# Stick-breaking keys on both partition halves: two score products of a unit in different rows of the array

## The chip, the cores and the metric

The kernel runs on one core of one Trainium2 chip. The time is device microseconds from the start to the end of one execution. Before the change three runs took 1735.06, 1747.95 and 1748.23 us, median 1747.95. The profiled execution took 1738.63 us, its span from the first to the last instruction 1736.7 us. Engines are called by their short names: PE is TensorE (matrix products and transposes), ACT is ScalarE, DVE is VectorE, POOL is GpSimd, SP issues DMAs.

## The reference

One layer of a hybrid encoder for 1,024 prompt rows and 64 sample rows. The rows are normed and projected to 2,464 columns. Three groups of heads read those columns; their outputs are joined, projected, added to the input, and followed by a gated MLP. The change lies in the third group, four heads of stick-breaking attention with 64 columns each:

```
zz = einsum("bqhd,bkhd->bhqk", q, k) * 64 ** -0.5
mask = k_pos < q_pos
log_beta = log_sigmoid(zz)
log_1mb = where(mask, log_beta - zz, 0)
after = cumsum(log_1mb, reverse=True) - log_1mb
w = where(mask, exp(log_beta + after), 0)
out = einsum("bhqk,bkhd->bqhd", w, v)
```

The prompt attends to itself. The sample's 64 rows attend to 512 cached keys and to their own 64. The sum over d, the inner dimension of the first product, has 64 terms: on PE this product uses 64 of the 128 rows of the array. All of it is fp32.

## The kernel before, in words

The program has three stages: norm and input projection (to 328 us), attention (328 to 800 us), output projection and MLP (the rest). Only the attention stage changes. Its order is written out by hand. There are nine turns: turn 0 is the sample, turns 1 to 8 are the prompt blocks of 128 queries. In turn n the prompt block looks at n x 128 keys, so turns 5 to 8 have more than 512 keys; they are called wide here. Each turn has twelve units, one per head: eight of the softmax group (M) and four stick-breaking (S), in the order S M M S M M S M M S M M.

Each unit passes through steps on all engines. In a step PE makes the scores of one unit (`scores`, lines 2001 to 2027), weighs the values of an earlier one (`weigh`, line 2071), transposes the weights of one between them (`transposes`, line 2051), and does one of twelve front pieces of the next turn (`front`). A front piece turns projected columns of the next block into the layouts that its units need. Piece 0 of each front transposes stick-breaking queries and keys into one PSUM bank; ACT copies the queries to `sqT` (line 1083), and DVE, after ACT, copies the keys to `skT` (line 1516). PE's next front pieces wait until both have read the bank where they share it. On ACT the copies of a front piece stand at the end of a step, ahead of the next step's exponentials and logarithms (lines 1135 to 1143) and of the copies of transposed weights (line 1163) that `weigh` on PE waits for. Before the first turn DVE copies the cached keys to `skT` (line 1481).

`sqT` and `skT` keep two heads on partitions 0 to 63 and two on partitions 64 to 127 (head h on half h % 2, at index h // 2). A score product reads keys and queries of one half. Since a product has at most 512 columns, a unit with more keys has two, into neighbouring PSUM banks, both from the half of its head. Turn 0 has two as well, 512 and 64 keys. A fp32 product leaves two weight-load records and two product records in the trace.

Before each front ACT squares and sums two column ranges of the next block into the two parts of a scratch tile `junk` (lines 1058 and 1060), and then makes their inverse roots.

Of the kernel before, what the change touches and what calls it, by code (L numbers as in the profile page):

```python
# [20 lines left out]
P = 128  # L21
# [154 lines left out]
def key_col(n):  # L176

    return P * SEQ[n]


# [94 lines left out]
def build(nc, I, O, stop_after=None):  # L275
# [4 lines left out]
    with ctx:  # L280
# [85 lines left out]
        qnT = s3("qnT", [3, P])  # L366
        junk = s3("junk", [QR + KVR])
        sums = s3("sums", [2])
# [12 lines left out]
        v_mla = s3("v_mla", [NTILE, 512])  # L381
        skT = s3("skT", [2, T])
        sv = s3("sv", [NTILE, 256])
        qT = s3("qT", [2, H_MLA, P])
        sqT = s3("sqT", [2, 2, P])
        prob = s3("prob", [3, 1024])
# [513 lines left out]
        def _(act):  # L900
# [150 lines left out]
            def prepare(m):  # L1051
# [4 lines left out]
                if m:  # L1056
                    act.wait_ge(s_lat, m)
                act.activation(junk[:r, :QR], x[:, O_ZQ:O_ZQ + QR], ACT.Square, scale=QR ** -0.5,
                               accum_out=sums[:r, 0:1])
                ch.link(act.activation(junk[:r, QR:], x[:, O_KV:O_KV + KVR], ACT.Square, scale=KVR ** -0.5,  # L1060
                                       accum_out=sums[:r, 1:2]))
# [3 lines left out]
            def front(m, p):  # L1065
# [16 lines left out]
                if s == 0:  # L1082
                    last = act.activation(sqT[:, slot, :, :r], v4[:, 0:2, :r], ACT.Copy, scale=SB_SCALE)
                elif s == 1:
# [217 lines left out]
        def _(dve):  # L1302
# [177 lines left out]
            dve.wait_ge(s_cT, 2)  # L1480
            dve.tensor_copy(skT[:, :, 512:1024], psum[:, 2:4, :]).then_inc(s_cD, 1)

# [21 lines left out]
            def front(m, p):  # L1504
# [10 lines left out]
                if s == 0:  # L1515
                    last = dve.tensor_copy(skT[:, :, col:col + r], v4[:, 2:4, :r])
                elif s in (2, 3):
# [256 lines left out]
        def _(pe):  # L1774
# [225 lines left out]
            def scores(i):  # L2000
# [17 lines left out]
                for a in range(0, w, 512):  # L2018
                    b = min(w, a + 512)
                    out = score_bank(i, w)[:r, a:b]  # L2020
                    if kind == "M":
                        last = pe.matmul(out, qT[:QD, slot, h, :r], kT[:QD, h, first + a:first + b],  # L2022
                                         start=True, stop=True)
                    else:
                        lo = 64 * (h % 2)
                        last = pe.matmul(out, sqT[lo:lo + 64, slot, h // 2, :r],  # L2026
                                         skT[lo:lo + 64, h // 2, first + a:first + b], start=True, stop=True)
                last.then_inc(s_sc, 1)
# [191 lines left out]
```

## Time and profile before

| what | value |
|---|---|
| runs | 1735.06, 1747.95, 1748.23 us |
| profiled execution | 1738.63 us, span 1736.7 us |
| mean granted clock of PE | 0.970 |
| busy PE / DVE / ACT / POOL | 1661.3 / 1063.3 / 609.0 / 169.8 us |
| stick-breaking score products (line 2026) | 112 records, 372.6 to 785.0 us |
| query copies `sqT` / key copies `skT` | 9 / 9, and 1 of the cached keys |

Busy time is the time in which an engine executed. A granted clock of 1.00 is PE's 2.4 GHz, 0.50 is 1.2 GHz. The chain of waits is followed back from the last instruction: at each step to what released it, or to the instruction ahead of it on its engine. An instruction with "idle before" had its engine waiting that long for the named releaser.

### The profile page before, as it was taken

The page shows a single profiled execution, that of the slowest core. Times are in us where ns is not written, and L with a number is a line of the kernel's source. Part 1 is how long each engine was busy: PE and PEld are TensorE (multiplying, and loading weights), DVE is VectorE, ACT ScalarE, POOL GpSimd, SP SyncE. Part 2 cuts the span into 40 slices and gives each one's busy share as a digit, 9 for nine tenths or more (in the row PEclk, how much of TensorE's full clock was granted, in tenths as well). Part 3 has the DMA queues.
Part 4 walks back from the last instruction along what each step waited for, and adds up shares of the span by engine and source line. Part 5 has one row for each costly group of instructions (what it writes and reads, how often), then busy time and mean ns, then how long its engine had stood idle before and what let it go on. Part 6 is the DMA issues. An engine that isn't in the chain of part 4 may idle for free.

```text
span 1736.7 us, 27549 instructions
## 1 busy us (share of the span) xinstructions
PE 1661.3 (96%) x10050; PEld 1497.0 (86%) x10050; DVE 1063.3 (61%) x2316; ACT 609.0 (35%) x1199; POOL 169.8 (10%) x226
## 2 busy tenths in 40 slices
PE   6899999899899999999998999999999999999996
PEld 3599999646676777777997999999999999999996
DVE  3766555346776676666327666665666666566657
ACT  4621000235666666666225222121212222121213
POOL 0011111212322212111210000000000000000000
PEclk8999999879988999999999999999999999999999
DMA  9545555511211110016210211111111211111003
GB/s 329 192 157 154 170 157 160 183 39 36 66 48 48 48 36 17 13 49 219 86 37 16 70 37 49 37 43 53 36 48 36 60 36 48 36 36 60 12 1 116
DMA packets 114221, 133.61 MB, mean 77 GB/s; under 512 B 14954, under 2 KB 91545, under 8 KB 112793
## 3 DMA queue, kind: packets, MB, share of 16 engines
q1 hardware_dynamic: 110809, 121.76, 22.0%
q0 software_dynamic: 3328, 10.73, 1.7%
q8 instruction: 53, 0.87, 0.2%
q14 instruction: 31, 0.25, 0.0%
HBM read 107.47 MB, written 27.23 MB: 78 GB/s over the span
## 4 chain that ended last, share of the span: by engine, by line
PE 86%; DVE 5%; ACT 5%; issue 3%; DMA 1%; SPq 0%; ACTq 0%; DVEq 0%; POOLq 0%
PE psum L2102 34%; PE psum L2166 15%; PE psum L1868 13%; PE psum L2071 6%; PE psum L2022 3%; PE psum L2051 3%; PE psum L2026 2%; PE psum L1954 2%; PE psum L1896 1%; PE psum L1901 1%; PE psum L1934 1%; PE psum L1782 1%; DVE h_lo L1422 1%; ACT pT L1163 1%; PE psum L1804 1%
## 5 line engine op out<-in xcount | busy, mean ns | idle before, releaser
L2102 PE MATMUL psum<-act_hi,wt_parts 128*128 128x362 f32 (+1 forms) x2496 | 614.4, 328 | 9.4 <-DVE act_lo L1422 5.2
L1718 DVE SCALAR_TENSOR_TENSOR residual<-psum,mod,residual 128x364 f32<-128x364 f32 (+2 forms) x704 | 299.7, 494 | 257.7 <-PE psum L2166 257.6
L2102 PEld LDWEIGHTS psum<-act_hi,wt_parts 128*128 128x128 f32 x2496 | 441.4, 189 | 12.1 <-issue 6.8
L2102 PE MATMUL psum<-act_lo,wt_parts 128*128 128x362 f32 (+1 forms) x1248 | 408.3, 327 | 0.0
L2166 PE MATMUL psum<-u_hi,wt_parts 128*128 128x362 f32 (+1 forms) x1056 | 263.3, 330 | 3.0 <-issue 3.0
L2102 PEld LDWEIGHTS psum<-act_lo,wt_parts 128*128 128x128 f32 x1248 | 235.0, 188 | 0.0
L2166 PEld LDWEIGHTS psum<-u_hi,wt_parts 128*128 128x128 f32 x1056 | 188.1, 189 | 3.3 <-issue 3.3
L1868 PE MATMUL psum<-w_hi,h_hi 128*128 128x308 f32 (+1 forms) x576 | 177.3, 308 | 3.9 <-DVE h_lo L1422 2.1
L1868 PE MATMUL psum<-w_lo,h_hi 128*128 128x308 f32 (+1 forms) x576 | 175.9, 305 | 0.0
L1868 PE MATMUL psum<-w_hi,h_lo 128*128 128x308 f32 (+1 forms) x576 | 175.4, 304 | 0.0
L2166 PE MATMUL psum<-u_lo,wt_parts 128*128 128x364 f32 (+1 forms) x528 | 174.6, 331 | 0.0
L1261 ACT ACTIVATE u_hi<-u_val 128x362 fp32r<-128x362 f32 (+1 forms) x66 | 33.4, 507 | 291.0 <-DVE u_val L1701 291.0
L1868 PEld LDWEIGHTS psum<-w_hi,h_hi 128*128 128x128 f32 (+1 forms) x576 | 105.7, 183 | 6.6 <-DVE h_lo L1422 2.6
L1240 ACT ACTIVATE a_ext<-psum 128x364 f32<-128x364 f32 (+1 forms) x88 | 32.1, 392 | 224.8 <-PE psum L2102 224.8
L2071 PEld LDWEIGHTS psum<-v_mla,pT 128*128 128x128 f32 (+1 forms) x656 | 80.8, 190 | 31.6 <-issue 20.2
L1868 PEld LDWEIGHTS psum<-w_lo,h_hi 128*128 128x128 f32 (+1 forms) x576 | 105.6, 183 | 0.4
L1868 PEld LDWEIGHTS psum<-w_hi,h_lo 128*128 128x128 f32 (+1 forms) x576 | 105.5, 183 | 0.4
L1163 ACT ACTIVATE pT<-psum 128x512 f32<-128x512 f32 (+3 forms) x156 | 69.6, 476 | 102.6 <-PE psum L2051 102.4
L1620 DVE TENSOR_TENSOR wt_parts<-wt_raw,wt_parts 128x1024 fp32r<-128x1024 f32 x74 | 91.0, 1232 | 22.0 <-ACT wt_parts L1184 22.0
L2166 PEld LDWEIGHTS psum<-u_lo,wt_parts 128*128 128x128 f32 x528 | 100.3, 190 | 0.0
L2071 PE MATMUL psum<-v_mla,pT 128*128 128x64 f32 (+1 forms) x656 | 82.4, 271 | 12.1 <-ACT pT L1163 9.8
L2022 PE MATMUL psum<-kT,qT 96*128 96x512 f32 (+4 forms) x224 | 87.7, 504 | 1.2 <-DVE zsb L1587 1.2
(227 smaller groups left out, 2172.4 us busy)
## 6 DMA issues: line engine op xcount, KB each, us to landing
wt_raw<-in_w_up SPq DMA_DIRECT2D x44, 512.0 KB, 3.8
ada_raw<-in_w_ada SPq DMA_DIRECT2D x32, 512.0 KB, 3.8
wt_raw<-in_w_down SPq DMA_DIRECT2D x22, 512.0 KB, 4.3
w_raw<-in_w_in SPq DMA_DIRECT2D x16, 616.0 KB, 5.6
z_scratch<-z_out POOLq DMA_DIRECT2D x64, 154.0 KB, 2.9
z_in<-z_scratch SPq DMA_DIRECT2D x8, 1232.0 KB, 5.3
ada_first<-in_w_ada SPq DMA_DIRECT2D x16, 512.0 KB, 11.5
xT_scratch<-xT SPq DMA_DIRECT2D x1, 4352.0 KB, 19.0
```

The source lines that it names most:

```text
L1163: last = act.activation(pT[:, wn % 4, :len(blocks), :r], src[:, :len(blocks), :r], ACT.Copy)\
L1261: act.activation(u_hi[:, slot, a:b], u_val[:, c % 2, :b - a], ACT.Copy).then_inc(s_uh, 1)
L1620: dve.tensor_tensor(wt_lo[:, slot], wt_raw[:, raw], wt_hi[:, slot].bitcast(F32), ALU.subtract)\
L1718: last = dve.scalar_tensor_tensor(out=res[:, d, a:b], in0=bank[4 + q % 4][:, a - CHUNKS[c][0]:b - CHUNKS[c][0]], scalar=mod[:, 40 + d, whi ...
L1868: last = pe.matmul(bank[t % 3][:r, 0:ZG], hh[:, k, P * t:P * t + r], ww[:, slot, k, :], start=(k == 0 and m == 0), stop=(k == KT - 1 and m ...
L1954: last = pe.matmul(b7[:r, 0:384], qnT[:, k, :r], w_uq[:, k, 384 * (s - 2):384 * (s - 1)], start=(k == 0), stop=(k == 2))
L2022: last = pe.matmul(out, qT[:QD, slot, h, :r], kT[:QD, h, first + a:first + b], start=True, stop=True)
L2026: last = pe.matmul(out, sqT[lo:lo + 64, slot, h // 2, :r], skT[lo:lo + 64, h // 2, first + a:first + b], start=True, stop=True)
L2051: last = pe.transpose(out[:size, P * k:P * k + r], src[:, col - first:col - first + size], ident[:r, :r])
L2071: last = pe.matmul(bank[pv_bank(v)][:r, 64 * (v % 8):64 * (v % 8) + 64], pT[:size, W_NO[x] % 4, k % 4, :r], vals, start=(k == 0), stop=(k ...
L2102: last = pe.matmul(out[:, :b - a], ww[:, slot, P * k:P * k + P], aa[:, k, a:b], start=(k == 0 and m == 0), stop=(k == KT - 1 and m == 2))
L2166: last = pe.matmul(bank[4 + q % 4][:, :b - a], ww[:, ring, P * d:P * d + P], uu[:, slot, a:b], start=(m == 0), stop=(m == 2))
```

## The change

Keys at positions 0 to 511 of the concatenated key axis stay on partitions 0 to 63, for all four heads; keys from 512 on go to partitions 64 to 127. In turn 0 all keys count from 512 on, and lie in the upper half. The queries are copied to the half or halves that their unit's keys use: the lower in turns 1 to 4, the upper in turn 0, both in turns 5 to 8. So the two products of a wide unit read different partitions and use different rows of the array. PSUM holds the transposed heads on two partition halves, and one copy can no longer write both: each query or key copy becomes one per source half, and in turns 5 to 8 the queries have one per source half and target half. `junk` is made smaller, and both squares write the same part of it, with a wait between them.

```diff
+def key_halves(n):
+    return ([1] if n == 0 else [0]) + ([1] if n > 4 else [])
...
-        junk = s3("junk", [QR + KVR])
+        junk = s3("junk", [QR])
...
-        skT = s3("skT", [2, T])
+        skT = s3("skT", [H_SB, 512 + LS])
...
-        sqT = s3("sqT", [2, 2, P])
+        sqT = s3("sqT", [2, H_SB, P])
...
-                act.activation(junk[:r, :QR], x[:, O_ZQ:O_ZQ + QR], ACT.Square, scale=QR ** -0.5,
-                               accum_out=sums[:r, 0:1])
-                ch.link(act.activation(junk[:r, QR:], x[:, O_KV:O_KV + KVR], ACT.Square, scale=KVR ** -0.5,
+                ch.link(act.activation(junk[:r], x[:, O_ZQ:O_ZQ + QR], ACT.Square, scale=QR ** -0.5,
+                                       accum_out=sums[:r, 0:1]))
+                ch.link(act.activation(junk[:r, :KVR], x[:, O_KV:O_KV + KVR], ACT.Square, scale=KVR ** -0.5,
                                        accum_out=sums[:r, 1:2]))
...
-                    last = act.activation(sqT[:, slot, :, :r], v4[:, 0:2, :r], ACT.Copy, scale=SB_SCALE)
+                    for b in key_halves(m):
+                        for a in range(2):
+                            last = act.activation(sqT[64 * b:64 * b + 64, slot, a:H_SB:2, :r],
+                                                  v4[64 * a:64 * a + 64, 0:2, :r], ACT.Copy, scale=SB_SCALE)
...
-            dve.tensor_copy(skT[:, :, 512:1024], psum[:, 2:4, :]).then_inc(s_cD, 1)
+            for a in range(2):
+                last = dve.tensor_copy(skT[64:128, a:H_SB:2, 0:512], psum[64 * a:64 * a + 64, 2:4, :])
+            last.then_inc(s_cD, 1)
...
-                    last = dve.tensor_copy(skT[:, :, col:col + r], v4[:, 2:4, :r])
+                    lo, at = 64 * (col // 512 > 0), col - 512 * (col // 512 > 0)
+                    for a in range(2):
+                        last = dve.tensor_copy(skT[lo:lo + 64, a:H_SB:2, at:at + r], v4[64 * a:64 * a + 64, 2:4, :r])
...
-                        lo = 64 * (h % 2)
-                        last = pe.matmul(out, sqT[lo:lo + 64, slot, h // 2, :r],
-                                         skT[lo:lo + 64, h // 2, first + a:first + b], start=True, stop=True)
+                        high = int(first + a >= 512)
+                        lo, at = 64 * high, first - 512 * high
+                        last = pe.matmul(out, sqT[lo:lo + 64, slot, h, :r], skT[lo:lo + 64, h, at + a:at + b],
+                                         start=True, stop=True)
```

ACT's instructions at the front of turn 8, before the change (`eg` is the gate, `stat` the group statistics, `esb` the stick-breaking unit, `pT` the transposed weights):

```order
L1075 ACTIVATE eg<-eg 128x256
L1083 ACTIVATE sqT<-psum 128x256
L1110 ACTIVATE stat<-stat,eps 128x4
L1111 ACTIVATE stat<-stat 128x4
L1135 ACTIVATE esb<-zsb 128x896
```

and with it:

```order
L1080 ACTIVATE eg<-eg 128x256
L1090 ACTIVATE sqT<-psum 64x2x128 x4
L1118 ACTIVATE stat<-stat,eps 128x4
L1119 ACTIVATE stat<-stat 128x4
L1143 ACTIVATE esb<-zsb 128x896
```

One copy became four, and all that follows stands behind them. DVE's instructions at the start of the attention stage, before (`w_uq_sb`, `mod` and `scale_n` are preparations, `lat` the latents of the first tile, `kT` the softmax keys):

```order
L1396 SCALAR_TENSOR_TENSOR scale_n<-mod,vec_a 128x16
L1481 COPY skT<-psum 128x2x512
L1500 TENSOR_SCALAR zqn<-z_in,rs 64x384
L1501 SCALAR_TENSOR_TENSOR lat<-z_in,rs,g_kv_sb 64x256
L1487 COPY kT<-psum 64x512
L1516 COPY skT<-psum 128x2x64
```

and with the change:

```order
L1404 SCALAR_TENSOR_TENSOR scale_n<-mod,vec_a 128x16
L1490 COPY skT<-psum 64x2x512 x2
L1510 TENSOR_SCALAR zqn<-z_in,rs 64x384
L1511 SCALAR_TENSOR_TENSOR lat<-z_in,rs,g_kv_sb 64x256
L1497 COPY kT<-psum 64x512
L1528 COPY skT<-psum 64x2x64 x2
```

Both key copies are doubled; the order is otherwise the same.

## Rows read from the trace of the kernel before

**Rows 1.** The page's engine table: busy us, share of the span, instructions.

```profile
PE 1661.3 (96%) x10050; PEld 1497.0 (86%) x10050; DVE 1063.3 (61%) x2316; ACT 609.0 (35%) x1199; POOL 169.8 (10%) x226
```

**Rows 2.** Stretches: us, busy PE, PEld, DVE, ACT, POOL, clock, DMA share, GB/s.

```profile
580.00:800.00 220.00, 212.70 (x1322) 161.27 (x1320) 151.09 (x322) 151.71 (x292) 45.15 (x39) 1.00 0.18 58
```

**Rows 3.** Chain of waits (start, us, what): units of turns 5, 6, 7, 8.

```profile
576.89 1.27 PE psum L2026 x4
...
626.79 1.48 PE psum L2026 x4
...
682.25 1.70 PE psum L2026 x4
...
756.19 1.91 PE psum L2026 x4
```

**Rows 4.** Timeline (start, us, engine, line): weight loads of a turn 8 unit.

```profile
743.62 0.19 PEld L2026 LDWEIGHTS psum<-skT,sqT 64*128 64x128 f32 x1 [0.24 <-issue]
744.04 0.19 PEld L2026 LDWEIGHTS psum<-skT,sqT 64*128 64x128 f32 x1 [0.24 <-issue]
```

**Rows 5.** Chain of waits, in the front of turn 8.

```profile
687.98 0.27 ACT sqT L1083
688.25 0.19 ACT stat L1110
...
692.12 0.58 ACT pT L1163
...
692.84 1.52 PE psum L2071 x12
```

**Rows 6.** Chain of waits, in the front of turn 5.

```profile
531.47 0.27 ACT sqT L1083
...
532.99 0.42 DVE skT L1516
...
534.94 1.34 PE psum L2071 x6
```

**Rows 7.** Chain of waits, at the start of the attention stage.

```profile
337.92 1.14 DVE skT L1481
...
341.00 0.30 DVE skT L1516
...
341.39 0.55 PE psum L1934 x3
```

**Rows 8.** Groups by form (busy us, mean ns), 340 to 820; one timeline row.

```profile
L1102 ACT ACTIVATE rqT<-psum 64x256 f32<-64x256 f32 x16 | 6.0, 378 | 3.2 <-PE psum L1934 3.0
...
L1586 DVE COPY zsb<-psum 128x512 f32<-128x512 f32 x4 | 2.8, 688 | 0.0
L1586 DVE COPY zsb<-psum 64x512 f32<-64x512 f32 x4 | 2.7, 675 | 0.0
...
699.88 0.76 ACT L1102 ACTIVATE rqT<-psum 64x256 f32<-64x256 f32 x2
```

**Rows 9.** Stretches around three waits of PE, columns as above.

```profile
532.00:535.00 3.00, 1.24 (x6) 0.44 (x4) 2.63 (x10) 2.94 (x7) 1.46 (x2) 1.00 0.28 53
535.00:549.00 14.00, 14.00 (x46) 10.03 (x47) 6.93 (x16) 7.02 (x16) 1.27 (x1) 0.51 0.26 96
581.00:586.00 5.00, 3.82 (x26) 2.82 (x25) 3.49 (x11) 4.88 (x12) 1.46 (x2) 1.00 0.41 118
586.00:600.00 14.00, 13.06 (x85) 10.04 (x85) 10.51 (x27) 9.56 (x23) 1.54 (x1) 1.00 0.19 67
793.00:797.00 4.00, 2.94 (x16) 1.66 (x14) 3.64 (x10) 3.97 (x6) 0.00 (x0) 1.00 0.94 258
798.00:805.00 7.00, 7.00 (x34) 6.41 (x33) 4.00 (x5) 3.04 (x6) 2.35 (x1) 0.52 0.02 5
```

**Rows 10.** Timeline, the squares of the first prompt tile.

```profile
361.24 0.19 ACT L1058 ACTIVATION_READ_ACCUMULATOR junk<-z_in 128x1 f32 x1
361.33 0.40 ACT L1060 ACTIVATE junk<-z_in 128x256 f32<-128x256 f32 x1
```

## Prediction

> **What bounds the kernel now.** I read the engine table of the page first. TensorE (PE) is busy for 96% of the span [rows 1]. The change touches only the attention stage, from 328 to 800 us, so I read the busy time of the engines by stretch next. In the wide part of the stage, 580 to 800 us, PE is busy for 212.7 of 220 us at a granted clock of 1.00, while DVE has 151.1 and ACT 151.7 [rows 2]. So an instruction saved on PE there is saved from the time, and ACT or DVE work costs nothing unless it sits in front of something PE waits for. The chain of waits says where that is. It runs through PE nearly everywhere, and leaves it at the start of the stage for DVE [rows 7] and once per turn, where the front of the next turn begins, for ACT [rows 5] or for ACT and then DVE [rows 6]. The change adds instructions in exactly these three kinds of place.
>
> **Part 1, the products of a wide unit (gain).** A stick-breaking unit of turns 5 to 8 has two products, over 512 keys and over the remaining 128, 256, 384 or 512. The chain shows such a unit at 1.27, 1.48, 1.70 and 1.91 us [rows 3]: 0.21 us for each further 128 keys. Each fp32 product leaves two records, two passes over its keys, so a pass over 128 keys costs 0.107 us and over 512 keys 0.43 us; the weight loads of the last two passes start 0.42 us apart (743.62 and 744.04) [rows 4], which confirms it. Now the four passes run one after another in the same 64 rows, although weights are loaded ahead. After the change passes 3 and 4 use the other 64 rows and another PSUM bank, so pass 3 may run beside pass 2. Passes 1 and 2 share rows, and so do 3 and 4, so I let them stay in order: the saving is the overlap of pass 2 (0.43 us) with what follows it. For 128 keys that is both short passes, 0.21 us; for 256 both, 0.43; for 384 and 512 it is limited by pass 2 itself, 0.43. Over four heads: 4 x (0.21 + 0.43 + 0.43 + 0.43) = **6.0 us**.
>
> No row of this trace has two neighbouring products in disjoint rows, so this is bounded from both sides: nothing at all (they go on in order as in [rows 4]), and the whole second product, 4 x (0.21 + 0.43 + 0.64 + 0.86) = 8.6 us. I take 6.0, which is nearest to what the rows show of the order of passes. The Trainium skill, "TensorE: Matmul & The Clock Gate", section "Measured speedup vs the span model", says that products in different row groups together last one product plus about 4 ns for each further tile; read for whole products that is 8.6 us less instead of 6.0, and no row here shows it. The turn of the sample (turn 0) has both its products in the upper half, and turns 1 to 4 have one product: nothing is gained there.
>
> **Part 2, the query copies on ACT (loss).** The one copy of 128 partitions x 256 becomes two of 64 partitions in turns 0 to 4 and four in turns 5 to 8. A copy of half the partitions is not cheaper: the existing 64x256 copy from PSUM takes 378 ns, and a pair of them 0.76 us [rows 8]; on DVE, 64x512 takes 675 ns and 128x512 688 [rows 8]. So each extra copy is 0.38 to 0.39 us of queue. In turn 8's front the chain goes through the query copy (0.27 us from its start to the next), the group statistics, three stick-breaking logs, one exponential, and the copy of transposed weights that PE waits for [rows 5]. ACT does not wait once in that stretch, so three more copies come out whole: 3 x 0.39 = 1.17 us. The fronts of turns 6 and 7 have the same shape, so 3 x 1.17 = **3.5 us**. In turn 5's front the same ACT copies come first, but the chain then crosses to DVE through the key copy [rows 6], which also doubles: 1.17 + 0.42 = **1.6 us**. In turns 1 to 4 only one copy is added, 0.39 us each; between 0 and 1.6 us, I take half, **0.8 us**, since the extra copy partly lies where ACT or DVE waits anyway.
>
> **Part 3, the key copies on DVE (loss).** The copy of the cached keys, 1.14 us of the chain, stands at the start of the stage with PE idle behind it, and so does the sample's key copy of 0.30 us [rows 7]. Both become two of the same free length: 1.22 + 0.3 = **1.5 us**, all on the path. In turns 6 to 8 the key copy grows by 0.42 us too, but there the chain goes through ACT, with the ACT copies as its cover; without that cover it would cost 0.42 each, 1.3 us together, about as much as ACT's share of one turn.
>
> **Part 4, the shared scratch tile (loss).** The two squares now write the same tile, so a wait stands between them. Behind it on ACT are the logarithm, the exponential and the query copies of that front. For the first prompt tile the second square starts at 361.33, 0.1 us before the first one's sum is read out at 361.43 (361.24 + 0.19) [rows 10]. It can no longer do so: **0.1 us** once, taken as on the path since PE is not far behind there. In later turns ACT is idle before they matter. PE, POOL and SP issue the same instructions as before, in the same order.
>
> **Part 5, the clock.** Where PE had been kept waiting, the granted clock fell behind it: after 1.24 busy of 3 us (532 to 535) it stood at 0.51 for 14 us with PE busy throughout, and after 2.94 of 4 us (793 to 797) at 0.52 for 7 us [rows 9]. Half speed (1.2 instead of 2.4 GHz) for L us of busy PE costs L/2: 7.0 and 3.5 us. In turn 6's front PE was busy for 3.82 of 5 us and the clock stayed at 1.00 [rows 9]. My extra 1.17 us of waiting makes that about 3.8 of 6.2, nearer to the first of the two cases that fell. The fronts of turns 7 and 8 are alike. I take two more short falls, out of three places: 2 x 3.5 = **7.0 us**. The bounds are 0 and three long ones, 21 us.
>
> **The sum.** -6.0 + 3.5 + 1.6 + 0.8 + 1.5 + 0.1 + 7.0 = +8.5 us. The profiled execution took 1738.6 us, so it would be 1747.1. That execution stands 9.3 us below the median of the three runs, 1747.95; two of the runs were at 1748, one at 1735. The four executions have a mean of 1742.5, and since each new one draws its own low-clock stretches I put the sum on that: **1751 us**. On the median itself it would be 1756.
>
> **The rivals.**
> - *No overlap in fp32.* The change would then not do what it says. For: no such pair is in the trace, and weights loaded ahead of a pass do not start it early now [rows 4]. Against: the banks differ and so do the rows. Price: 8.5 + 6.0 = +14.5, 1757 us. Chance 0.28.
> - *Overlap, and the clock holds.* For: turn 6's front kept 1.00 with a wait of this kind [rows 9]. Price: +1.5, 1744 us. Chance 0.20.
> - *Whole products side by side.* -8.6 instead of -6.0, and no fall: -1, 1741 us; were the 14 us stretch behind 535 also gone, 1734. It would need pass 3 to start with pass 1, past pass 2 in the queue. Chance 0.05.
> - *Slower.* Each of the three lengthened fronts is followed by a low stretch like the one after 535 (14 us, 7.0 us lost): 3 x 7.0 replaces 7.0, so +22.5, 1765 us, 1.3% over the mean before; without overlap 1771. It decides from the point where PE's wait in the front of turns 6 to 8 becomes as long as the 1.76 us of turn 5's front (3 - 1.24 busy) and the work behind it keeps PE waiting at the lower clock. Against it: after 797 the low stretch lasted 7 us, not 14 [rows 9]. Chance 0.07.
> - The forecast itself: overlap of one pass, two short falls. Chance 0.40.
>
> About 1% (17 us) is what a measurement of this kernel can tell from no change; the runs before already span 0.8%. The forecast and three rivals lie within it. Slower by more than 1% takes the last rival and a part of the first with longer falls: 0.07 + 0.04 = 0.11. Faster by more than 1% needs 1725 us, which no combination here reaches without losing several low stretches by luck: 0.03. Same: 0.86. Range for 8 in 10: from 1738, under the overlap case by the spread of the runs, to 1764, over the no-overlap case by two more short falls.
>
> **What the changed profile would show.** Overlap right: in a wide unit of turn 8 the third pass's record starts well under 0.43 us after the second's, and the unit's chain piece falls from 1.91 to about 1.5 us; the score products of turns 1 to 4 are unchanged. ACT right: 17 more query copies near 0.38 us each, four in a row in the fronts of turns 5 to 8, and PE's wait for the copy of transposed weights in those fronts about 1.2 us longer. DVE right: two 64x1024 copies of about 1.2 us before the first transposes of the stage, which start 1.5 us later. Clock right: stretches near 0.5 behind 585, 637 or 694. The forecast is wrong if third passes keep their 0.43 us (then about 6 us more), if PE's waits in the fronts do not grow (then about 5 us less, and the falls go with them), or if the low stretches come elsewhere, which this one execution cannot foretell.

## The result and the profile after

| | before | after |
|---|---|---|
| runs of the comparison, us | 1735.06, 1747.95, 1748.23, 1730.92 | 1756.94, 1750.66, 1768.04, 1765.78 |
| median, us | 1741.5 | 1761.4 |
| profiled execution, us (span) | 1738.63 (1736.7) | 1756.94 (1755.3) |
| mean granted clock of the profiled execution | 0.970 | 0.961 |

The ratio on record is 1.0138, 95% interval [1.0102, 1.0174]; the plain quotient of the two medians of four is 1.0114. The kernel is slower by 1.4%. Forecast was a difference too small to be measured, 1751 us, with a range from 1738 to 1764, and a loss of more than 1% had a chance of 0.11. The time lies in the range, but by luck: the range was built on a level of 1742.5 us for the kernel before, and 66 later runs put it at 1735.1. The upper end is 21.5 us above the level that it was built on, and the loss is 24 us.

The engine table of after, the same columns as [rows 1]:

```profile
PE 1666.1 (95%) x10050; PEld 1504.4 (86%) x10050; DVE 1068.3 (61%) x2326; ACT 619.3 (35%) x1216; POOL 169.8 (10%) x226
```

ACT has 17 more instructions and 10 us more busy time, DVE 10 more and 5 us. PE has as many as before, and is busy 4.8 us longer in a span that is 18.6 us longer. So PE waits more, and the work that it does takes longer although each wide unit became shorter.

**The products do run side by side.** The chain of waits, two units of turn 8 (start, us, what), which answer to the last of [rows 3]:

```profile
772.95 1.06 PE psum L2039 x4
...
786.66 1.06 PE psum L2039 x4
```

And the score product's line between 799 and 800 us, one unit of turn 8 (count, then duration in ns: shortest, median, longest, then first and last start):

```profile
L2039 PEld LDWEIGHTS psum<-skT,sqT x4: 182/184/186, 799.1 to 799.2; 64*128 64x128 f32 x4
L2039 PE MATMUL psum<-skT,sqT x4: 589/641/693, 799.1 to 799.7; 64*128 64x512 f32 x4
```

The unit took 1.91 us and takes 1.06. All four weight loads start within about 0.1 us, where those of the last two passes stood 0.42 us apart in [rows 4]. The first passes of the two products start at 799.119 and 799.125 us by their records, the second passes at 799.652 and 799.659: the products go pass by pass together, 6 to 7 ns apart. Units of turns 5, 6 and 7 take 1.05 to 1.06 us as well (1.27, 1.48 and 1.70 before). The saving is 4 x (0.21 + 0.43 + 0.64 + 0.86) = 8.6 us.

**The fronts wait longer.** ACT and DVE in the front of turn 6 (start, us, engine, line, what, idle before); rows between are left out:

```profile
591.02 1.53 ACT L1090 ACTIVATE sqT<-psum 64x256 f32<-64x256 f32 x4
592.58 0.30 ACT L1118 ACTIVATE stat<-stat,eps 128x4 f32<-128x4 f32 x1
592.92 0.21 ACT L1119 ACTIVATE stat<-stat 128x4 f32<-128x4 f32 x1
```

```profile
593.16 0.42 DVE L1573 TENSOR_TENSOR oc<-oc,stat 128x256 f32<-128x256 f32 x1 [2.30 <-ACT stat L1119]
...
594.07 0.86 DVE L1528 COPY skT<-psum 64x256 f32<-64x256 f32 x2
```

Four query copies take 1.53 us, where one took 0.27 to its successor [rows 5]. DVE stands idle for 2.30 us behind them, since it scales the retention heads with the statistics that ACT makes after the copies. Only then come the two key copies, 0.86 us. PE's next front piece needs the bank that both read. Its waits in the fronts of turns 6, 7 and 8, after:

```profile
595.03 0.52 PE L1946 MATMUL psum<-ident_sb,zqn 128*128 128x128 f32 x3 [2.57 <-issue]
...
650.20 0.52 PE L1946 MATMUL psum<-ident_sb,zqn 128*128 128x128 f32 x3 [2.03 <-issue]
...
708.46 0.52 PE L1946 MATMUL psum<-ident_sb,zqn 128*128 128x128 f32 x3 [1.42 <-issue]
```

and before, turns 6 and 7 (turn 8 had none there):

```profile
583.52 0.52 PE L1934 MATMUL psum<-ident_sb,zqn 128*128 128x128 f32 x3 [0.82 <-issue]
...
634.02 0.52 PE L1934 MATMUL psum<-ident_sb,zqn 128*128 128x128 f32 x3 [0.59 <-issue]
```

The waits grew by 1.75, 1.44 and 1.42 us. Part of it comes back at PE's next wait, the one for the transposed weights. In the same three fronts it stood at 0.36, 0.57 and 0.79 us before:

```profile
585.48 1.07 PE L2071 MATMUL psum<-v_mla,pT 128*128 128x64 f32 x8 [0.36 <-ACT pT L1163]
...
636.41 1.30 PE L2071 MATMUL psum<-v_mla,pT 128*128 128x64 f32 x10 [0.57 <-ACT pT L1163]
...
692.84 1.52 PE L2071 MATMUL psum<-v_mla,pT 128*128 128x64 f32 x12 [0.79 <-ACT pT L1163]
```

After, there is none in turns 6 and 7, where PE works at half clock by then, and 0.37 us in turn 8:

```profile
710.86 1.52 PE L2084 MATMUL psum<-v_mla,pT 128*128 128x64 f32 x12 [0.37 <-ACT pT L1171]
```

Both waits together grew by 1.39, 0.87 and 1.00 us, 3.3 us in all.

**The clock falls behind them.** Stretches of after, the columns of [rows 2] (each row ends with the granted clock, the DMA share and GB/s):

```profile
425.00:439.00 14.00, 13.72 (x69) 10.92 (x70) 8.13 (x29) 8.86 (x31) 2.17 (x4) 0.52 0.31 108
592.00:596.00 4.00, 1.43 (x10) 0.98 (x9) 2.69 (x7) 3.84 (x9) 1.45 (x2) 1.00 0.25 64
596.00:606.00 10.00, 10.00 (x40) 7.71 (x40) 6.45 (x14) 4.15 (x11) 1.54 (x1) 0.50 0.35 126
...
650.70:657.50 6.80, 6.80 (x26) 5.00 (x25) 4.48 (x11) 4.07 (x11) 0.13 (x1) 0.50 0.55 206
...
710.00:725.00 15.00, 14.13 (x87) 10.21 (x86) 10.40 (x22) 12.42 (x25) 2.08 (x1) 1.00 0.00 1
811.00:821.00 10.00, 9.97 (x47) 9.70 (x48) 4.85 (x8) 4.01 (x8) 2.35 (x1) 0.51 0.30 82
```

PE was busy for 1.43 of 4 us in the front of turn 6, and then worked for 10 us at 0.50, busy throughout, with ACT busy for 4.15 us of it. The front of turn 7 is followed by 6.8 us at 0.50, that of turn 8 by none. Before, 580 to 800 us stood at 1.00 as a whole, but for the fall at its end [rows 2, 9]. Two low stretches that both kernels have are alike or longer: 13.7 us after the front of turn 5 in both, and 10.2 us at the end of the stage for 6.8. One is new that I had not named: 13.7 us at 425, in turn 2. Before, the same stretch stood at full clock:

```profile
425.00:439.00 14.00, 13.38 (x96) 9.85 (x95) 10.14 (x42) 10.00 (x37) 3.19 (x8) 1.00 0.41 128
```

It is no accident of one execution. All five profiles of kernels with doubled query copies in turns 1 to 4 have a low stretch there (13.7 us in after, in after again and in two variants of after below, 6.8 us with the ACT copies alone), and none of the other eight profiles has one between 400 and 440 us.

Added up, the profiled execution of after has 137 us at the low clock, and before 105. One execution is a poor witness of this, though. Each run has its span and its mean granted clock, and 2 x (1 - clock) x span is its time at the low level. Over 66 runs of before that stood beside the experiments the mean is 89 us, and the mean time 1735.1 (two more, of 3819.76 and 4103.39 us, are left out, at over twice the time of any other). Over ten runs of after (these four and six more below) it is 143 us and 1759.5. So 24.5 us of time go with 54 us more of the low clock. Had PE been the bound all through these stretches, that would be 27 us. Comparing each run only with runs of its own kernel (171 runs of 12 kernels), the time grows by 0.35 us for each us at the low clock, 0.27 to 0.48 by kernel; that makes 19 us. What remains for everything else is between -2 and +6 us.

### The profile page after: what moved, and what is told of

Its sections match the earlier page's. It is cut to its first block, busy times and chain, and to the rows that moved or that the text cites. A ratio compares the mean times of both kernels' runs of the same rounds, so it can differ in the third digit from the quotient of the medians.

```text
span 1755.3 us, 27576 instructions
## 1 busy us (share of the span) xinstructions
PE 1666.1 (95%) x10050; PEld 1504.4 (86%) x10050; DVE 1068.3 (61%) x2326; ACT 619.3 (35%) x1216; POOL 169.8 (10%) x226
## 4 chain that ended last, share of the span: by engine, by line
PE 86%; ACT 5%; DVE 5%; issue 3%; DMA 1%; SPq 0%; ACTq 0%; DVEq 0%; POOLq 0%
PE psum L2115 34%; PE psum L2179 15%; PE psum L1880 12%; PE psum L2084 6%; PE psum L2034 3%; PE psum L2064 3%; PE psum L1966 2%; PE psum L2039 2%; PE psum L1908 1%; PE psum L1913 1%; PE psum L1946 1%; PE psum L1794 1%; DVE h_lo L1430 1%; ACT pT L1171 1%; PE psum L1816 1%
## 5 line engine op out<-in xcount | busy, mean ns | idle before, releaser
L2084 PEld LDWEIGHTS psum<-v_mla,pT 128*128 128x128 f32 (+1 forms) x656 | 86.0, 201 | 34.9 <-issue 24.7
L2084 PE MATMUL psum<-v_mla,pT 128*128 128x64 f32 (+1 forms) x656 | 87.6, 283 | 14.9 <-ACT pT L1171 14.7
```

Of the source, the lines that this page charges most:

```text
L2084: last = pe.matmul(bank[pv_bank(v)][:r, 64 * (v % 8):64 * (v % 8) + 64], pT[:size, W_NO[x] % 4, k % 4, :r], vals, start=(k == 0), stop=(k ...
```

## The experiments

Two theories stood first. The waits theory (W): side-by-side products are a gain of 8.6 us, the doubled copies are the loss, by PE's longer waits at the fronts and by the clock that falls behind them. The rows theory (R): the products in alternate rows cost something themselves, in their neighbourhood or through the clock. A third, on phase (P), came up after the first runs: a small shift early in the stage moves the low stretches, whatever the copies at the fronts do. All times below are medians, and the ratios are to before on the same chip, as recorded; the quotient of two medians can differ from them by up to 0.2%.

| kernel | median us | ratio [95%] | low clock, mean us |
|---|---|---|---|
| after again | 1759.67 | 1.0147 [1.0118, 1.0177] | 140 |
| after, both products in the lower rows | 1771.46 | 1.0202 [1.0181, 1.0223] | 149 |
| before + ACT copies | 1757.01 | 1.0126 [1.0105, 1.0146] | 127 |
| before + DVE copies | 1748.78 | 1.0077 [1.0047, 1.0108] | 120 |
| before + only the cached-key copy in two | 1736.37 | 1.0007 [0.9992, 1.0021] | 93 |
| after + PE work ahead of the fronts' wait | 1752.81 | 1.0108 [1.0074, 1.0141] | 121 |
| other rows, late query copies | 1744.61 | 1.0042 [1.0015, 1.0068] | 117 |
| the same + scores ahead | 1740.83 | 1.0044 [1.0028, 1.0060] | 115 |
| late copies + later weight split | 1733.24 | 0.9998 [0.9979, 1.0016] | 97 |
| before + later weight split | 1736.02 | 1.0003 [0.9985, 1.0021] | 94 |
| late copies + scores ahead + later weight split | 1730.22 | 0.9959 [0.9938, 0.9981] | 89 |

### After without the side-by-side products

Both products of a wide unit read the lower 64 partitions, the second with the keys of the first 512 positions, so its scores are of the wrong keys; in the sample's turn both read the upper ones.

```diff
-                        high = int(first + a >= 512)
-                        lo, at = 64 * high, first - 512 * high
+                        high = int(n == 0)
+                        lo, at = 64 * high, first - 512 * int(first + a >= 512)
```

> The changed kernel, except that the second product of a wide unit reads queries and keys of the lower half again (of the first 512 positions, so its scores are of the wrong keys); every copy is as in the changed kernel. Theory W (the added copies lengthen PE's waits in the fronts, and these waits bring the low clock; the overlap of products is a plain gain): the wide units take 1.27 to 1.91 us again instead of 1.05, so 16 units give back 4 x (0.21 + 0.43 + 0.64 + 0.86) = 8.6 us: about 8 us slower than the changed kernel, near 1.8% over the kernel before. Theory R (side-by-side products leave PE too little to do, and that brings the low clock): no slower than the changed kernel, at most 1.4% over before, with fewer low stretches than the 137 us of the changed kernel.

The ratio is 1.0202: slower than after. R falls as a cause of loss. A unit of turn 8 in its chain of waits is back at the length of before:

```profile
796.09 1.91 PE psum L2039 x4
```

Against after again (1.0147) that is 0.55%, 9.5 us, which the two intervals leave open by some 6 us; the units' arithmetic says 8.6, and 9 us more of the low clock could add some 3. So the worth of the products side by side agrees with what the profile says, and the copies cost about 2%.

### The copies on ACT alone

Before, with two 64-partition query copies in place of one, and in turns 5 to 8 two more into a spare tile `sqX`. The products stay as they were.

```diff
-                    last = act.activation(sqT[:, slot, :, :r], v4[:, 0:2, :r], ACT.Copy, scale=SB_SCALE)
+                    for out in [sqX[:, :, :r]] * int(m > 4) + [sqT[:, slot, :, :r]]:
+                        for a in range(2):
+                            last = act.activation(out[64 * a:64 * a + 64], v4[64 * a:64 * a + 64, 0:2, :r],
+                                                  ACT.Copy, scale=SB_SCALE)
```

> The kernel before, with only ACT's query copies as in the changed kernel: two 64x256 copies in turns 0 to 4, four in turns 5 to 8 (the extra pair goes to a tile that nothing reads). Theory W: PE's wait for the second front piece in the fronts of turns 6 to 8 grows from 1.0, 0.8 and 0 us by about 1.2 us each, turn 5's front too, low stretches follow one or two of them: 8 to 14 us slower than before (0.5 to 0.8%). Theory R: no products are side by side, so at most the 4.7 us of waits, 0.3%, and low stretches as before (105 us).

1.0126, 22 us, more than W expected of them (8 to 14). PE's waits for the second front piece in turns 6, 7 and 8 are 2.12, 1.90 and 1.35 us, 1.30 to 1.35 longer than before. The stretches around the front of turn 6 show where it goes (columns as above):

```profile
581.00:585.20 4.20, 2.50 (x16) 1.69 (x14) 1.75 (x6) 4.01 (x12) 0.00 (x0) 0.99 0.01 2
585.20:598.90 13.70, 13.28 (x45) 10.09 (x46) 7.76 (x17) 6.87 (x16) 2.98 (x3) 0.50 0.33 111
```

PE was busy for 2.50 of 4.2 us there, and 13.7 us at 0.50 follow, in a place where before stays at 1.00 [rows 9]. Seventeen copies of 0.38 us are 6.5 us of ACT; the time grew by over three times as much. This kernel has the new stretch in turn 2 too (6.8 us at 424.7), with one extra copy there.

### The copies on DVE alone

Before, with each key copy in two halves of 64 partitions, the cached keys' too.

```diff
-                    last = dve.tensor_copy(skT[:, :, col:col + r], v4[:, 2:4, :r])
+                    for a in range(2):
+                        last = dve.tensor_copy(skT[64 * a:64 * a + 64, :, col:col + r], v4[64 * a:64 * a + 64, 2:4, :r])
```

> The kernel before, with only DVE's key copies doubled (two of 64 partitions in place of each one of 128, the cached keys too). Theory W: 1.5 us at the start of the stage, and 0.42 us in series with ACT in the fronts of turns 5 to 8, 1.7 us together: 3 us slower, 0.2%, with no more low stretches. Theory R: the same, for the same reason. A third theory, that the second key copy is what decides since the bank is freed behind it, would give over 8 us (0.5%).

1.0077, 13 us. W had 3 us, 0.42 in each of four fronts and 1.5 at the start, so it missed; the third theory on record, over 8 us because the bank is freed behind the second key copy, has the size. The waits themselves came out as W had them. For the second front piece of turns 6, 7 and 8:

```profile
585.15 0.52 PE L1937 MATMUL psum<-ident_sb,zqn 128*128 128x128 f32 x3 [1.36 <-issue]
...
635.99 0.52 PE L1937 MATMUL psum<-ident_sb,zqn 128*128 128x128 f32 x3 [1.14 <-issue]
...
691.92 0.52 PE L1937 MATMUL psum<-ident_sb,zqn 128*128 128x128 f32 x3 [0.48 <-issue]
```

They are 0.54, 0.55 and 0.48 us longer than before. At full clock, PE's next wait, for the transposed weights, gave back 0.36, 0.57 and 0.43 of that, and turn 5's wait is 1.76 us in both kernels. The profile has no low stretch at the fronts of turns 6 to 8. So neither the waits nor falls at these fronts make the 13 us. Together with the last one it makes 1.26 + 0.77 = 2.03%, within the intervals the 2.02% of all the copies without side-by-side products. The profiled execution shows one stretch that [rows 9] have at 7 us:

```profile
795.00:799.10 4.10, 3.03 (x19) 1.99 (x18) 3.15 (x8) 3.88 (x6) 0.00 (x0) 1.00 0.99 267
799.10:829.80 30.70, 28.32 (x123) 26.60 (x123) 10.34 (x20) 14.04 (x26) 2.35 (x1) 0.50 0.20 76
```

Once fallen at the end of the stage, the clock stayed at 0.50 for 30.7 us, behind a wait of 1.07 us; before, a wait of 1.06 us was followed by 6.8. The mean low time is 31 us above before's, of which 0.35 to 0.5 per us gives 11 to 15 us. So the size is that of the clock. Which of the DVE copies brings it, and how, I can't say from this run: none of them stands near 795 us.

### Only the copy of the cached keys

```diff
-            dve.tensor_copy(skT[:, :, 512:1024], psum[:, 2:4, :]).then_inc(s_cD, 1)
+            for a in range(2):
+                last = dve.tensor_copy(skT[64 * a:64 * a + 64, :, 512:1024], psum[64 * a:64 * a + 64, 2:4, :])
+            last.then_inc(s_cD, 1)
```

> The kernel before, with only the copy of the cached keys in two (one instruction more in the whole program, 1.2 us). Theory W: 1.2 to 1.5 us slower, 0.08%, low clock as before. Theory P: this shift of everything behind it by 1.2 us moves the waits of the fronts against the clock's windows, and gives part of the 13 us that all key copies together cost: 4 us or more, 0.25% up.

1.0007 [0.9992, 1.0021]. A shift of the whole stage by 1.2 us changes the time by about itself and no more, so P falls for a shift at the start of the stage, and the loss comes from the copies at the fronts. Whether DVE's act there by PE's waits or by shifting what follows, this run can't tell. One of its 13 runs took 1747.06 us, and that one is profiled. Again it is the end of the stage:

```profile
797.80:828.50 30.70, 28.32 (x123) 26.60 (x121) 10.94 (x21) 14.64 (x26) 2.35 (x1) 0.50 0.24 93
```

The wait ahead of it is 1.06 us, as in before. So a long stretch there also comes in a kernel that is as good as before; the other 12 runs, at most 1738.91 us, leave little room for one. Runs of before itself near 1748 us may be the same thing; none of them was profiled.

### After again

> The changed kernel once more, beside the next three. Theory W: between the 2.02% of the kernel without the overlap and the 2.03% that the two kinds of copies sum to, less the 8.6 us of the overlap: 1.4 to 1.6% over before, 1760 to 1763 us, with about 50 us more of low clock than before. Theory P (the low clock comes and goes with the moment at which waits fall, whatever their length): a value anywhere from 0.5 to 2%, with single runs 10 us apart.

1.0147, six runs with a mean of 1759.0: the loss stands in a second set of runs. Its profile has the same low stretches as after, 13.7 us at 427, 10.2 at 598, 6.8 at 653 and 10.2 at 813.

### PE kept at work during the wait

After, with the score products of the next unit issued twice in turns 6 to 8: once ahead of the front piece that waits for the bank, as mere filling, and again where they stood.

```diff
+                if s == 1 and 5 < m < NTILE:
+                    scores_filler(step + 1)
                 if m < NTILE:
                     front(m, s)
```

> The changed kernel, with PE kept busy in its longest waits: ahead of the second front piece of turns 6, 7 and 8 (waits of 2.7, 2.2 and 1.6 us) it first makes the next unit's softmax scores, 1.25 to 1.7 us of products into the bank where they are made again, properly, right after. The added products do nothing useful. Theory W, the clock being the larger part: the low stretches behind 596 and 651 (10.2 and 6.8 us) go, so 6 to 9 us faster than the changed kernel beside it. If waits as such are the cost and the clock is only a companion: no faster, or 1 us slower. Theory P: no difference that holds over the runs.

PE does more work and the kernel gets faster: 1752.81, 6.9 us less than after again beside it, as W expected; the two intervals overlap a little, so the size is not firm. The place is. With the filling:

```profile
593.00:598.00 5.00, 3.41 (x21) 2.54 (x21) 2.58 (x7) 4.85 (x11) 1.46 (x2) 1.00 0.18 33
598.00:608.00 10.00, 9.19 (x62) 6.85 (x61) 8.42 (x21) 7.35 (x17) 1.53 (x1) 1.00 0.37 137
653.00:660.00 7.00, 6.46 (x46) 4.96 (x45) 5.98 (x11) 5.12 (x13) 1.81 (x1) 1.00 0.07 21
```

and after again, without it:

```profile
594.00:598.00 4.00, 1.45 (x12) 1.13 (x11) 2.41 (x6) 3.86 (x9) 1.46 (x2) 1.00 0.22 41
598.00:608.00 10.00, 10.00 (x40) 7.59 (x39) 6.73 (x15) 4.39 (x11) 1.54 (x1) 0.52 0.37 135
653.00:660.00 7.00, 7.00 (x27) 4.99 (x25) 4.72 (x11) 4.30 (x11) 0.10 (x1) 0.51 0.56 201
```

In the same 10 us behind the front of turn 6, PE starts 62 product records at 1.00 and 40 at 0.52. The copies and their length are untouched here, and only PE's idle time is filled: this ties these low stretches to PE's waits and not to the copies as such. The 10.2 us at the end of the stage are gone too (3.4 us at 827 are left), and the 13.7 us in turn 2, ahead of all filling, stay.

### Other rows, with the copies off the path

If the products are worth 8.6 us and the copies cost 2%, the copies must leave the path. This kernel keeps before's layout. Only the keys of turns 5 to 8 are written to the opposite half (two DVE copies), and only there the queries are copied once more, from SBUF to the other half (`sqX`), as two ACT copies in front piece 4, later than PE's wait. `junk` is cut as in after.

```diff
+                if p == 4 and m > 4:
+                    for a in range(2):
+                        act.activation(sqX[64 - 64 * a:128 - 64 * a, slot, :, :r], sqT[64 * a:64 * a + 64, slot, :, :r],
+                                       ACT.Copy).then_inc(s_sx, 1)
...
-                    last = dve.tensor_copy(skT[:, :, col:col + r], v4[:, 2:4, :r])
+                    if m > 4:
+                        for a in range(2):
+                            last = dve.tensor_copy(skT[64 - 64 * a:128 - 64 * a, :, col:col + r],
+                                                   v4[64 * a:64 * a + 64, 2:4, :r])
...
-                        lo = 64 * (h % 2)
-                        last = pe.matmul(out, sqT[lo:lo + 64, slot, h // 2, :r],
+                        other = int(n > 0 and first + a >= 512)
+                        lo = 64 * (h % 2 ^ other)
+                        last = pe.matmul(out, (sqX if other else sqT)[lo:lo + 64, slot, h // 2, :r],
```

> The same overlap with fewer and later copies. Keys and queries stay where the kernel before has them; only the keys of turns 5 to 8 are written to the other half (two key copies there, one elsewhere and for the cached keys), and the swapped queries are made from the finished query tile by two ACT copies four front pieces later, off the place where PE waits. Theory W: the gain of 8.5 us stays, the cost is 0.42 us in four fronts, so 5 to 8 us faster than before (ratio 0.995 to 0.997) and low stretches near those of before. Theory R: the overlap brings the low clock, so not faster than before (1.000 or more), with low stretches well over 105 us.

1.0042: by the ratios 1.0% better than after, but not faster than before, so W missed, and R's forecast came out (the variants below tell them apart). Of its twelve runs four took 1730.72 to 1732.69 us, one 1739.30, and seven 1744.40 to 1751.19. The profiled one, 1732.27, kept the clock where before lost it, and lost it elsewhere:

```profile
533.00:537.00 4.00, 2.24 (x16) 1.44 (x14) 3.45 (x11) 3.87 (x10) 1.45 (x2) 1.00 0.43 123
537.00:550.00 13.00, 12.68 (x71) 8.64 (x70) 10.21 (x27) 9.47 (x22) 1.27 (x1) 1.00 0.22 82
784.00:788.60 4.60, 2.69 (x13) 1.41 (x12) 4.45 (x8) 4.54 (x6) 0.68 (x1) 1.00 1.05 266
788.60:799.00 10.40, 10.40 (x49) 9.81 (x49) 4.72 (x8) 4.24 (x8) 2.36 (x1) 0.51 0.27 78
```

and before, ahead of its 14 us at 0.51 [rows 9]:

```profile
532.00:536.00 4.00, 2.24 (x11) 1.44 (x10) 3.52 (x12) 3.78 (x9) 1.46 (x2) 0.89 0.44 138
```

PE is busy for 2.24 of 4 us in both fronts, and the clock falls in one and holds in the other. So the length of the wait alone does not decide whether the clock falls.

At the end of the stage ACT is busy for 4.54 of 4.6 us while PE waits, 1.91 us for the transposed weights where before waits 1.06. My reading is that units that got faster have moved PE closer to ACT there, and ACT carries besides the first three splits of the output projection's weights.

### Scores ahead of the front's wait

In turns 6 to 8 the real scores of the next unit come ahead of the second front piece, instead of a filling.

```diff
+                if s == 1 and 5 < m < NTILE:
+                    scores(step + 1)
```

> The variant with swapped halves and late query copies, and on PE the next unit's scores of turns 6 to 8 issued ahead of the second front piece, in place of behind it, so the waits of 1.4, 0.9 and 0.3 us there are filled with useful products. Theory W: 2 to 3 us less waiting and fewer low stretches, so 5 to 10 us faster than that variant, 0.2 to 0.5% faster than before (1727 to 1732 us). Theory P: like the variant, runs split between 1731 and 1749.

1740.83, a miss of some 10 us; the ratio is that of the variant without it. The end of the stage, profiled:

```profile
784.00:787.40 3.40, 1.48 (x8) 0.68 (x6) 3.25 (x8) 3.37 (x6) 0.00 (x0) 1.00 1.13 281
787.40:821.50 34.10, 31.72 (x138) 30.00 (x138) 11.82 (x24) 16.13 (x29) 2.36 (x1) 0.50 0.28 100
```

PE waits there for 1.92 us of 3.4, as long as in the variant without it (1.91), with ACT busy for 3.37, and 34.1 us at 0.50 follow where that execution had 10.4. The end of the stage can take back what the fronts gain.

### The weight splits five steps later

ACT and DVE split the first three weight tiles of the output projection in steps 103 to 105, among the last units of the stage. One number moves them behind the units.

```diff
-EARLY_SPLIT = 103
+EARLY_SPLIT = 108
```

With the late copies:

> The variant with swapped halves and late query copies, and the early splits of three projection weights (ACT 1.06 us and DVE 1.49 us each) at steps 108 to 110 in place of 103 to 105, so behind the last scores. In that variant PE's longest wait, 2.1 us before 788.5 us, stood in the last score step with ACT waiting for DVE, and a low stretch came behind it; its runs split between 1731 and 1749 us. Theory W: that wait shrinks to about 1 us or less and the slow group of runs goes: 1728 to 1733 us, 0.2 to 0.4% faster than before. Theory P: runs still split in two groups 15 us apart, median near 1742.

1733.24, 0.9998, so as fast as before and not 0.2 to 0.4% faster; the group of runs around 1749 is gone, the slowest of twelve is 1739.89. PE's wait there is 0.73 us instead of 1.91. The products are side by side here as well, and the low time is 97 us against 117: R falls as an account of the late copies' result. With before alone, as control:

> The control: the kernel before with the three early splits at steps 108 to 110, nothing else. Its wait there is 1.2 us before 796 us. Theory W: a little of that wait goes, and the splits themselves delay the projection's start by up to 3 us: between 2 us faster and 2 us slower. Theory P: the same.

1.0003: in before the splits are in nobody's way, so the 0.44% that it gives to the late copies is a cost which the faster units had brought up. With late copies and the scores ahead:

> Both on top of the swapped halves with late copies: scores of turns 6 to 8 issued ahead of the second front piece, and the early splits at steps 108 to 110. Theory W: the best of all, 1724 to 1730 us, 0.3 to 0.6% faster than before. Theory P: like the others of this family, about 1740 us.

1730.22, ratio 0.9959 [0.9938, 0.9981], twelve runs from 1720.57 to 1732.73, near the expected time. It is the one version that beats both kernels: by 0.4% over before (0.2% by the medians, 0.3% by the means) and, by the ratios, some 1.8% over after. Its profile behind the front of turn 6 and at the end of the stage:

```profile
596.00:606.00 10.00, 8.74 (x53) 6.17 (x52) 6.11 (x16) 7.42 (x19) 6.33 (x9) 1.00 0.18 53
...
785.00:789.00 4.00, 3.96 (x28) 3.00 (x26) 2.38 (x6) 2.55 (x6) 0.00 (x0) 1.00 0.10 23
789.00:810.00 21.00, 16.46 (x112) 15.38 (x113) 12.77 (x21) 15.33 (x28) 2.35 (x1) 0.84 0.53 175
```

At 785, PE is busy for 3.96 of 4 us, and the clock stands at 1.00; a fall comes later and is short, 6.8 us. The mean low time is 89 us, that of before. So its gain of 6 us in the means fits the shorter units less the copies that are left, 8.6 - 4 x 0.42 = 6.9; that sum was not tested by itself.

## Why the prediction was wrong, point by point

**The step that failed is Part 5, the clock.** Its 7.0 us ("two more short falls, out of three places") should have been 19 to 27. At the three fronts that it names it was nearly right: 10.2 and 6.8 us of low clock, none at the third, at most 8.5 us for the 7.0 in the sum. Two things went wrong around it. It looked for falls only where turns 6 to 8 wait, and the profiled execution has 13.7 us more in turn 2 and 3.4 us more at the end of the stage; three other kernels had 30.7 to 34.1 us there. The stretch in turn 2 comes with the one extra query copy of a narrow front, which Part 2 had priced at 0.39 us. And it took the clock of one execution as the state before: that one had 105 us at the low level, where 66 runs have a mean of 89. So the two profiles differ by 32 us at the low clock, and the means by 54. The sum itself was +8.5 us for a measured 24: that the forecast of 1751 missed by only 10 us is owed to its level, 7 us too high. The slower rival, with long falls, stood at 1765 us with a chance of 0.07, and the time came near it (1761); its mechanism did so in part, at other places than the three that it names.

**Part 1** erred the other way. I took an overlap of one pass, 6.0 us; whole products run side by side, 8.6. The rival had 0.05 because "it would need pass 3 to start with pass 1, past pass 2 in the queue", and that is what the records show: 799.119 and 799.125. The order of passes in [rows 4] was no evidence, since all of them share rows there. The Trainium skill had it right ("TensorE: Matmul & The Clock Gate", "Measured speedup vs the span model": together such products last one product and about 4 ns for each further tile); the trace agrees in kind, for fp32 with its two passes, with 6 to 7 ns in place of the 4. The Trainium skill, "TensorEngine Tiling (Array Packing)", section "Key Properties", says besides that different tiles load weights and multiply in parallel, which the four loads within about 0.1 us at 799.1 agree with.

**Part 2** had the number and the length of the copies right, and their cost at the wide fronts. By form, after:

```profile
L1090 ACT ACTIVATE sqT<-psum 64x256 f32<-64x256 f32 x24 | 9.0, 376 | 3.3 <-PE psum L1946 3.1
```

The row has 24 of the 26 copies; those of the sample are of another shape. In the fronts of turns 6 to 8 PE's two waits together are 3.3 us longer, for 3.5. **The cover in Part 3** held on balance, but not at the wait where it matters for the clock. ACT's copies stand ahead of the key copies in series, through the statistics that DVE waits for (2.30 us at 593.16), so the wait for the second front piece grew by both, up to 1.75 us. I had read [rows 5], where the chain goes through ACT only, and not what DVE waited for there. But the next wait, for the transposed weights that ACT copies, shrinks by much of what PE has already waited: in turn 8, at full clock in both kernels, 1.00 us is left for the 1.17 of Part 2, and with the DVE copies alone about 0.1 us in turns 7 and 8. Turn 5's wait grew from 1.76 to 3.22 us, 1.5 for the 1.6, but not by the path of Part 2: the chain runs through the query copies on ACT, and the key copies alone leave the wait at 1.76.

**Part 3 at the start of the stage** was right in the copies. The chain of waits there, after:

```profile
337.01 1.22 DVE skT L1490
338.24 0.53 DVE skT L1490
...
341.95 0.28 DVE skT L1528
342.25 0.30 DVE skT L1528
342.64 0.55 PE psum L1946 x3
```

The two copies of the cached keys take 2.46 us for 1.22 and the sample's 0.59 for 0.29, 1.5 together. PE's first transposes start at 342.64 for 341.39 [rows 7], 1.25 us later; that is not the copies alone, since DVE began them 0.91 us earlier in this execution (337.01 for 337.92) and took 0.5 us longer over `lat` between them. **Part 4**, 0.1 us, is too small to be seen in any of these runs.

**Without the clock** the corrected terms give -8.6 + 3.3 + 1.5 + 0.8 + 1.5 + 0.1 = -1.4 us, in which the 0.8 and the 0.1 are still the forecast's. The runs allow -2 to +6 for that. So the direct effects nearly cancel, as forecast (+1.5), and most or all of the loss goes with the clock.

**What stays open.** Whether the clock's share is 19 or 27 us. How the stretch in turn 2 comes about: it goes with the doubled query copies, but PE's waits around 425 are alike in both profiles (0.75 us), and longer with the ACT copies alone (1.29 for 0.62). And why the copies on DVE alone cost 0.77%: their low-clock time fits it, but the fronts' waits do not, and which of the copies sets it off was not tried.

## What to carry to other kernels

Two fp32 products that read different halves of the partitions and write different PSUM banks ran side by side here, pass by pass; price them at the length of the longer one. Then price what it takes to get operands there by which wait of TensorE each copy stands ahead of: follow both engines to it in series, take in the next wait, which may shrink by as much, and put the copy where TensorE does not wait. In this kernel waits of 1 to 3 us were followed by 7 to 34 us at half clock, or by none, so count low-clock time over many runs of both kernels, not in one profile of each, and after making TensorE faster look for the next queue it will run into.

## What the runs showed of the hardware

- Two fp32 products in different 64 rows start 6 to 7 ns apart, in both of their passes, and a unit of 2 x 512 keys goes from 1.91 to 1.06 us.
- The same wait, PE busy for 2.24 of 4 us, was followed by 14 us at 0.51 in one execution and by 13 us at 1.00 in another kernel's.
- A fall at the end of the attention stage lasted 30.7 to 34.1 us in three profiled executions, with PE busy for over 90% of it, and 6.8 and 10.2 us in others; a wait of 1.06 to 1.07 us stood ahead of 6.8 us in one and of 30.7 us in two.
- Between runs of the same kernel (12 kernels, 171 runs) time grew by 0.35 us for each us that the clock stood at its low level, not by the 0.5 of a PE that is always the bound.
- A copy from PSUM of 64 partitions x 256 takes 376 ns on ACT, one of 128 x 256 366 ns (median, before); two copies of 64 x 1024 on DVE take 2.46 us where one of 128 x 1024 took 1.22.
- More work on PE made a kernel faster (1752.8 for 1759.7 us), where it filled a wait.
